# Differential attention: the copy of the first turned chunk of each step moved from VectorE to ScalarE

## What is computed

```python
def block(i):                       # one block of 128 queries
    s = jnp.einsum('bqhcd,bkhcd->bhcqk', qb, k).astype(jnp.float32) * scale
    causal = kpos[None, :] <= qpos[:, None]
    p = jax.nn.softmax(jnp.where(causal, s, -jnp.inf), axis=-1)
    a = p[:, :, 0] - lam * p[:, :, 1]
    return jnp.einsum('bhqk,bkhe->bqhe', a.astype(v.dtype), v)
```

## Time and profile before

| | |
|---|---|
| median of 3 runs | 2474.91 us (2472.2 to 2475.5) |
| the profiled execution, its own time | 2475.9 us |
| span of the profiled execution (first to last instruction) | 2474.1 us |
| mean granted TensorE clock | 0.996 of full |
| TensorE matmul busy | 2443.0 us, 99% |
| VectorE busy | 1417.7 us, 57% |
| ScalarE busy | 985.2 us, 40% |
| GpSimd busy | 193.8 us, 8% |
| differential attention's steps | about 1552 to 1612 us of the span |

### The profile page before, as it was taken

How to read it: one execution, slowest core, us unless ns; L and a number is a source line. 1 busy time by engine, 2 the same in 40 slices (tenths; PEclk the granted TensorE clock), 3 DMA queues, 4 the chain that set the end, 5 groups by cost and what they waited for, 6 DMA issues and landing times.

```text
span 2474.1 us, 33205 instructions
## 1 busy us (share of the span) xinstructions
PE 2443.0 (99%) x11780; PEld 1942.9 (79%) x11780; DVE 1417.7 (57%) x2359; ACT 985.2 (40%) x1715; POOL 193.8 (8%) x326
## 2 busy tenths in 40 slices
PE   9999999999999999999999999899999999999999
PEld 7877787888887876788888787678887568888887
DVE  5765437777426346677752688746647764442432
ACT  4333424433313346443331444734336753431331
POOL 0000000000001013000000110300102540000000
PEclk9999999999999999999999999999999999999999
DMA  4322232333332320333333232042222003332333
GB/s 134 86 77 77 77 106 83 94 100 100 113 94 77 94 77 10 94 102 94 102 111 95 86 97 86 10 152 73 81 74 64 1 10 102 92 95 94 98 98 102
DMA packets 278503, 210.90 MB, mean 85 GB/s; under 512 B 12229, under 2 KB 234098, under 8 KB 278386
## 3 DMA queue, kind: packets, MB, share of 16 engines
q1 hardware_dynamic: 270465, 198.64, 27.2%
q10 hardware_dynamic: 7920, 10.70, 1.3%
HBM read 207.22 MB, written 2.10 MB: 85 GB/s over the span
## 4 chain that ended last, share of the span: by engine, by line
PE 84%; issue 7%; DVE 3%; ACT 2%; DVEq 1%; POOLq 1%; POOL 1%; DMA 0%; ACTq 0%
PE PS L161 15%; PE PS L162 15%; PE PS L163 15%; PE PS L158 10%; PE PS L160 10%; PE PS L159 10%; PE PS L1583 2%; PE PS L1603 2%; PE PS L1612 2%; ACT PB L1654 1%; POOLq L2300 1%; PE PS L2388 1%; DVE TT L737 1%; ACT WH L149 1%; DVEq L673 0%
## 5 line engine op out<-in xcount | busy, mean ns | idle before, releaser
L154 DVE TENSOR_TENSOR WL<-RAW,WH 128x1024 fp32r<-128x1024 f32 x352 | 431.2, 1225 | 709.4 <-ACT WH L149 702.7
L149 ACT ACTIVATE WH<-RAW 128x1024 fp32r<-128x1024 f32 x354 | 374.6, 1059 | 979.5 <-PE PS L160 552.3
L161 PE MATMUL PS<-XH,WH 128*128 128x512 f32 x1512 | 594.6, 393 | 3.7 <-DVE WL L545 2.1
L163 PE MATMUL PS<-XH,WL 128*128 128x512 f32 x1512 | 589.3, 390 | 0.0
L162 PE MATMUL PS<-XL,WH 128*128 128x512 f32 x1512 | 589.0, 390 | 0.0
L161 PEld LDWEIGHTS PS<-XH,WH 128*128 128x128 f32 x1512 | 284.1, 188 | 68.6 <-issue 5.6
L163 PEld LDWEIGHTS PS<-XH,WL 128*128 128x128 f32 x1512 | 284.1, 188 | 59.9
L162 PEld LDWEIGHTS PS<-XL,WH 128*128 128x128 f32 x1512 | 284.2, 188 | 58.1 <-issue 1.0
L158 PE MATMUL PS<-WH,XH 128*128 128x512 f32 x384 | 153.6, 400 | 0.2
L160 PE MATMUL PS<-WL,XH 128*128 128x512 f32 x384 | 150.8, 393 | 0.0
L159 PE MATMUL PS<-WH,XL 128*128 128x512 f32 x384 | 150.6, 392 | 0.0
(11 more groups left out here) (502 smaller groups left out, 3783.2 us busy)
## 6 DMA issues: line engine op xcount, KB each, us to landing
RAW<-in_ffn_w_up SPq DMA_DIRECT2D x88, 512.0 KB, 3.7
RAW<-in_w_in SPq DMA_DIRECT2D x60, 512.0 KB, 3.5
RAW<-in_ffn_w_down SPq DMA_DIRECT2D x44, 512.0 KB, 3.6
RAW<-in_sc_ssm_w_in SPq DMA_DIRECT2D x42, 512.0 KB, 3.7
RAW<-in_w_mlp_up SPq DMA_DIRECT2D x32, 512.0 KB, 3.9
RAW<-in_w_mlp_down SPq DMA_DIRECT2D x32, 512.0 KB, 3.6
RAW<-in_fox_w_in SPq DMA_DIRECT2D x24, 512.0 KB, 3.7
RAW<-in_sc_ssm_w_out SPq DMA_DIRECT2D x16, 512.0 KB, 3.6
```

The costliest lines, as they stand in the source:

```text
L149: act.activation(WH[:, slot, :], RAW[:, slot, :], ACT.Copy).then_inc(hi_ready, 1)
L154: dve.tensor_tensor(WL[:, slot, :], RAW[:, slot, :], WH[:, slot, :], ALU.subtract).then_inc(lo_ready, 1)
L161: pe.matmul(o, wh, ah, start=first, stop=False)
L163: return pe.matmul(o, wl, ah, start=False, stop=last)
```

## The change

ScalarE copies chunk 0 of head t-1 too, directly after the output copy of head t-2 and directly ahead of its copy of chunk 1; VectorE's copy is gone. The new copy raises the same semaphore `pd`, so that TensorE's waits are untouched, and it waits for the same two things as the old one, now in ScalarE's queue. Nothing else is moved.

```diff
@@ diff_act
                 act.activation(OD[:, :, (t - 2) * P:(t - 1) * P],
                                PS[:, OUT, :].rearrange("p (c d) -> p c d", c=NC_), ACT.Copy).then_inc(da.oa, 1)
             if 1 <= t <= KT:
+                act.activation(*diff_copy(act, t - 1, 0), ACT.Copy).then_inc(da.pd, 1)
                 act.activation(*diff_copy(act, t - 1, 1), ACT.Copy).then_inc(da.pa, 1)
             if t < KT:
                 pair_exps_act(act, da, t, 2, PBD)
@@ diff_dve
                 pair_masked_dve(dve, da, t, 1, PBD, ROWMASK, 3)
             if t == 2:
                 lo(dve, bd, 0, 0, 23)
-            dve.tensor_copy(*diff_copy(dve, t - 1, 0)).then_inc(da.pd, 1)
             if t < KT:
                 diff_combine_dve(dve, t, 0)
                 pair_masked_dve(dve, da, t, 2, PBD, ROWMASK, 3)
```

## The result

| | before | after |
|---|---|---|
| median of 20 runs each | 2474.54 us | 2477.77 us |
| lowest to highest | 2472.20 to 2478.09 | 2473.62 to 2481.56 |
| ratio after to before, 95% interval | | 1.0014 (1.0008 to 1.0020) |
| profiled execution: own time, span, mean clock | 2475.9, 2474.1, 0.996 | 2476.6, 2474.8, 0.998 |

The interval is +2.0 to +4.9 us, the medians +3.2 us; 2477.6 us was forecast. By the bound set in the prediction (0.2%) it is no change that can be told, but with this many runs the interval lies wholly on the slow side. That 2477.6 and 2477.77 lie so close is luck: the forecast stood on a median of three runs that was 0.4 us above that of twenty, and the measured shift is 0.6 us larger than the 2.67 us forecast.

What follows compares the result with a forecast made beforehand. TensorE bounds nearly everything, but differential attention is set by a ring of waits across engines; 0.27 (step 2) + 1.92 (steps 3 to 6) + 0.48 (step 7) = 2.67 us longer, 2477.6 us against the median, range 2474.0 to 2481.0.

Steps and rivals of the forecast that it cites:

- The ring: Steady differential-attention step: waits circling ScalarE, VectorE, GpSimd, VectorE set its 7.38 us; the new copy lies on it; chance 0.77.
- (a): Eight copies removed from VectorE, 0.61 us of queue each: its waits grow, the steady step does not shorten, worth 0.
- (b): Eight copies added to ScalarE between exps(t,1) and exps(t,2): 0.48 us per step, bounds 0 and 0.57.
- (c): ScalarE's new wait for turned chunk 0: TensorE's transposes of it start 2.5 us earlier or more, cost 0.
- (d): First step (t=1): the copy fits in ScalarE's 1.44 us idle before its copy of chunk 1, cost 0.
- (g): Last step (t=8): ScalarE's last copy ends 1.9 us before TensorE needs it, so one more costs 0.
- (e): Second step (t=2): VectorE was the later one; ScalarE's longer queue brings the reciprocal at 1566.70 against 1566.43, +0.27 us.
- (f): Steps 3 to 6 lengthen by 1.92 us through the ring, step 7 by 0.48 us through chunk 2's copy.
- (h): After the stage: no DMA moves, and TensorE's few remaining waits cannot take the delay in.
- Rival 3: TensorE's clock falls in steady steps as the values-products wait widens to about 1.56 us: +3.9 us per fallen step; chance 0.08.
- the lead of 0.78 us: TensorE's branch in a fallen steady step: a lead of 0.30 + 0.48 us, reducing the fall's cost from +4.7 to +3.9.

Runs made afterwards that it cites:

- the three moves: Kernel before with output copy ahead of exps(t,1), exps(t,2) ahead of chunk 1's copy, VectorE's copy behind masked(t,2), scores(t,2) ahead of values products: 0.9996.
- the extra copy: Kernel before with one more 128x512 ScalarE copy ahead of its copy of chunk 1, VectorE keeping its own copy: 1.0014.

## Why the prediction was right

- **The ring** held in the changed kernel and in the runs that add a copy to it or take one off. Moving a copy of 0.48 us on, twice on, or off it moves the period by 0.48, by 0.9 to 1.0 and back by 0.43 to 0.48. Where the order was changed more (the exponentials first, the three moves) the reckoned period was 0.4 to 0.5 us too short each time, because another ring, which I had not added up, closed later.
- **(a) VectorE's copy is worth 0**: 0.05 us a steady step, by the run that cut it to 8 columns; its waits took up the rest. In step 2 it is worth 0.30 us by itself, which ScalarE's longer queue takes away again: with the extra copy step 2 is 7.88 us, in the changed kernel 7.86.
- **(b) 0.48 us per step**: 0.485 measured. The nearest rows in the same queue were the right price, not the 0.57 us duration.
- **(c), (d), (g), no cost**: ScalarE has no wait before line 2260 in any step, and the last step lost 0.03 us. In step 1 ScalarE's old wait for TensorE (1.44 us) is gone in the profile after, taken up by the new copy and by the shorter low clock together. At a like clock step 1 is 7.84 to 7.92 us in the other profiles, with the copy on ScalarE or on VectorE, so (d) holds to 0.1 us.
- **(e) step 2**: +0.26 against +0.27, from a wait that changed sides: VectorE's reciprocal, which was late by itself, now waits 0.79 us for ScalarE.
- **(f)**: +1.94 and +0.49 against 1.92 and 0.48.
- **(h) nothing takes the delay in after the stage**: the waits of TensorE there are the same to 0.1 us.
- **Rival 3** was mispriced, and its way in was overlooked. I asked only whether the wait of 1.56 us in the steady steps lowers the clock; it did not, in any profile. The falls began in step 2, behind a wait of 1.18 us that the prediction does not have, in one of four profiled executions of the changed kernel, and went on behind waits of 2.2 us. A fallen step costs 0.7 us and not 3.9: the low level held for the values products alone (4.1 us for 2.5), not for the whole of TensorE's part, and the lead of 0.78 us, which was right, covers half of that. A larger chance at a smaller price hardly moves the forecast. The +3.2 us of the medians holds whatever such falls add in 20 runs; the 2.7 us of the ring alone are seen in the profiles only.
- The copy is shorter on ScalarE, 0.57 to 0.58 us against 0.69, and the step still became longer. The placement that the Trainium skill states (VectorE: DVE Perf Modes, Specifications: ScalarE sits closer to PSUM) speaks for the move; the rows agree with it on the copy, and the step goes the other way.

## What to carry to other kernels

Before a piece of work is moved to a less busy engine, follow the ring of waits once round and ask whether its new place lies on it: an engine that is idle for a fifth of the step may be idle only because it waits for its own last result. The same copy costs its full queue time there, nothing in the idle time before the ring's head, and part of it off the first ring, where a second one soon closes. Add up every ring that passes the engine, the one through its whole queue among them, before trusting a reordering.

## What the runs showed of the chip that I had not expected

TensorE's clock fell although TensorE was busy for some 80% of each step: behind waits of 1.18 to 2.40 us, in a stage of small products, and not in every execution of the same kernel with the same waits. Six waits of 1.91 to 2.40 us were each followed by a fall, sixteen of 1.49 to 1.57 us by none, and those of about 1.18 us in step 2 by a fall in two executions of five. Once the clock has fallen, the wait two steps later is longer, and it falls again. It also fell with TensorE busy all the time: in the kernel before, 64 products of 32 columns each, from 1812 to 1816 us, are followed by a granted clock of 0.73 and 0.84 in two stretches of 4 us. The Trainium skill, TensorE: Matmul & The Clock Gate, section HAM oscillation, puts such falls down to idle gaps; the rows of the first kind agree with it in that each fall stands behind a wait, these here show a fall without a gap.

```profile
1810.00:1814.00 4.00, 4.00 (x43) 3.34 (x41) 0.45 (x1) 1.52 (x2) 0.00 (x0) 1.00 0.18 69
1814.00:1818.00 4.00, 4.00 (x43) 3.55 (x42) 3.66 (x8) 1.45 (x2) 0.00 (x0) 0.73 0.43 131
1818.00:1822.00 4.00, 4.00 (x16) 3.20 (x15) 1.65 (x4) 0.63 (x1) 0.00 (x0) 0.84 0.00 0
```

Such stretches come and go between executions of one kernel, at 12, 966, 1550, 1815 and 1832 us, about 1.6 us each where TensorE is busy all the time (behind the stage, by fourteen profiles), and 0.7 us in these steps, where its lead covers part. One of them is more than half of what this change costs, and they are the reason why its 2.7 us could be read from the steps of one profile to 0.05 us, but from the whole times only with 20 runs.
